# Two transformer blocks in split fp32: the order of the high and low matmuls inside a weight unit

## What is computed

```
def swiglu(h, w_gate, w_up, w_down):
    return (jax.nn.silu(h @ w_gate) * (h @ w_up)) @ w_down
...
proj = h @ w_in
...
return jnp.concatenate([o_attn, o_gla], axis=-1) @ w_out
```

## Time and profile before

| | |
|---|---|
| time, median of 3 runs | 3454.76 us (3454.75 to 3456.53) |
| the profiled execution's own time | 3454.76 us |
| its span, first to last instruction | 3452.9 us |
| TensorE matmul busy | 3390.2 us, 98% of the span |
| TensorE weight load busy | 2946.1 us, 85% |
| VectorE busy | 2366.0 us, 69% |
| ScalarE busy | 1726.5 us, 50% |
| DMA engines, mean busy share | 55% |
| mean granted TensorE clock | 0.994 of full speed |

### The profile page before, as it was taken

One profiled execution on the slowest core, in us unless ns is written; L12 is line 12 of the kernel. 1 busy time (PEld: TensorE's weight loads), 2 busy tenths in 40 slices (PEclk: granted clock), 3 DMA queues, 4 the chain that ended last, 5 costly groups with the idle time before them and its releaser, 6 DMA issues.

```text
span 3452.9 us, 59148 instructions
## 1 busy us (share of the span) xinstructions
PE 3390.2 (98%) x19584; PEld 2946.1 (85%) x19584; DVE 2366.0 (69%) x3637; ACT 1726.5 (50%) x2503; POOL 408.3 (12%) x442
## 2 busy tenths in 40 slices
PE   8999999999999999999999999999999999999999
PEld 7888888887888878888888888888888888888888
DVE  7666666676766856666666677886666668666666
ACT  5444444455444645444444466764444446454454
POOL 1000000011122301000000011210333331101100
PEclk9999999999999999999999999999999999999999
DMA  6665666564554644666566665555554455454545
GB/s 227 187 197 184 192 189 186 177 185 128 152 157 148 194 141 148 193 189 185 186 192 188 187 191 168 187 177 182 152 150 148 146 152 178 152 162 141 162 143 159
DMA packets 167930, 592.48 MB, mean 172 GB/s; under 512 B 18320, under 2 KB 22672, under 8 KB 167712
## 3 DMA queue, kind: packets, MB, share of 16 engines
q1 hardware_dynamic: 166688, 587.11, 55.0%
q10 hardware_dynamic: 1152, 4.19, 0.3%
HBM read 589.14 MB, written 2.10 MB: 171 GB/s over the span
## 4 chain that ended last, share of the span: by engine, by line
PE 50%; issue 11%; DVE 4%; ACT 2%; POOL 1%; DVEq 0%; ACTq 0%; POOLq 0%
PE bank L398 30%; PE bank L397 8%; PE bank L400 7%; PE bank L599 2%; DVE w_low L1218 1%; PE bank L613 1%; POOL rstd L1780 1%; DVE normed L1263 1%; ACT w_high L809 1%; POOL work L1828 1%; DVE residual L1253 0%; DVE increment L1250 0%; PE bank L484 0%; PE bank L491 0%; PE bank L497 0%
## 5 line engine op out<-in xcount | busy, mean ns | idle before, releaser
L398 PE MATMUL bank<-normed,w_high 128*128 128x512 f32 x6208 | 2026.7, 402 | 13.8 <-DVE w_low L1218 10.0
L1218 DVE TENSOR_TENSOR w_low<-w_raw,w_high 128x1024 fp32r<-128x1024 f32 (+1 forms) x1120 | 1372.4, 1234 | 480.6 <-ACT w_high L809 458.3
L809 ACT ACTIVATE w_high<-w_raw 128x1024 fp32r<-128x1024 f32 (+1 forms) x1120 | 1166.1, 1043 | 620.4 <-PE bank L398 601.3
L398 PEld LDWEIGHTS bank<-normed,w_high 128*128 128x128 f32 x6208 | 966.9, 189 | 23.4 <-issue 17.6
L397 PE MATMUL bank<-normed,w_low 128*128 128x256 f32 x3104 | 866.6, 279 | 0.0
L400 PE MATMUL bank<-normed,w_low 128*128 128x256 f32 x3104 | 863.4, 278 | 0.0
L398 PE MATMUL bank<-mixed,w_high 128*128 128x512 f32 x2496 | 796.2, 397 | 6.6 <-DVE increment L1250 6.3
L397 PEld LDWEIGHTS bank<-normed,w_low 128*128 128x128 f32 x3104 | 584.6, 188 | 141.9
L400 PEld LDWEIGHTS bank<-normed,w_low 128*128 128x128 f32 x3104 | 586.5, 189 | 133.9 <-issue 7.7
L826 ACT ACTIVATE parts<-bank 128x256 f32<-128x256 f32 x520 | 198.2, 381 | 822.4 <-PE bank L398 822.3
L1241 DVE TENSOR_TENSOR increment<-bank,parts 128x256 f32<-128x256 f32 x388 | 164.3, 423 | 342.8 <-ACT parts L826 342.5
(11 more groups left out here) (245 smaller groups left out, 2155.1 us busy)
## 6 DMA issues: line engine op xcount, KB each, us to landing
w_raw<-w_hg SPq DMA_DIRECT2D x128, 512.0 KB, 3.5
w_raw<-w_att SPq DMA_DIRECT2D x128, 512.0 KB, 3.6
w_raw<-w_up1a SPq DMA_DIRECT2D x64, 512.0 KB, 4.1
w_raw<-w_up1b SPq DMA_DIRECT2D x64, 512.0 KB, 3.9
w_raw<-w_up2a SPq DMA_DIRECT2D x64, 512.0 KB, 4.1
w_raw<-w_up2b SPq DMA_DIRECT2D x64, 512.0 KB, 4.1
w_raw<-w_rg SPq DMA_DIRECT2D x64, 512.0 KB, 4.3
w_raw<-w_up1c SPq DMA_DIRECT2D x48, 512.0 KB, 4.0
```

The costliest lines, as they stand in the source:

```text
L398: last = nc.tensor.matmul(banks[b][:, :], hi, x, start=starts and k == 0, stop=stop)
L809: A_(wh[slot][:, 0:width], raw[slot][:, 0:width], ACT.Copy).then_inc(wh_done, 1)
L1218: TT(wl[slot][:, 0:width], raw[slot][:, 0:width], wh[slot][:, 0:width].bitcast(F32), ALU.subtract).then_inc(wl_done, 1)
```

## The change

Within a unit every tile now does high, then low, whatever its number. The one exception is the last tile of a unit that closes a group, which does low, then high. The number of matmuls, their operands and their weight loads are the same; only their order inside a unit differs.

```
-                        stop = stops and k == nk - 1
-                        if t % 2:
+                        if stops and k == nk - 1:
                             nc.tensor.matmul(banks[b][:, 0:S], lo, x[:, 0:S], start=False, stop=False)
-                        last = nc.tensor.matmul(banks[b][:, :], hi, x, start=starts and k == 0, stop=stop)
-                        if t % 2 == 0:
+                            last = nc.tensor.matmul(banks[b][:, :], hi, x, start=False, stop=True)
+                        else:
+                            nc.tensor.matmul(banks[b][:, :], hi, x, start=starts and k == 0, stop=False)
                             last = nc.tensor.matmul(banks[b][:, 0:S], lo, x[:, 0:S], start=False, stop=False)
                         t += 1
```

## The result

The changed kernel takes 3481.28 us (median of 4 runs, 3478.25 to 3482.65), the kernel before 3454.76 us in the same comparison (3454.08 to 3456.53). The ratio is 1.0073, 95% interval 1.0061 to 1.0085: 25 us slower (the two medians lie 26.5 us apart, the two profiled executions 24.8). Of 21 executions of the changed kernel on record, one took 5422 us at a mean granted clock of 0.58 and isn't counted. The forecast was 3454.8 us, no change, with a range up to 3478; the result lies 3 us above that range. The profiled execution of the changed kernel took 3479.54 us.

What follows compares the result with a forecast made beforehand. The prediction took TensorE's stream of matmuls to bound the kernel. Reordering was counted as 0: 3454.76 + 0 = 3454.8 us, no change within 0.2% (chance 0.47), range 3438 to 3478 us.

Steps and rivals of the forecast that it cites:

- What bounds the kernel: Whole kernel: as long as TensorE's matmul stream, matmul row busy 3390.2 of 3452.9 us; main-stream tiles 3032 us, 88%.
- The count of turned rounds: Main stream: 3736 of 4352 two-tile rounds turn from L L H H into L H L H.
- the sensitivity: Main stream: 1 ns more a round lengthens the kernel by 3.7 us; 1.85 ns a round is needed to be seen.
- The counts 8088 and 616: Profile sign: lines 397 and 400 trade places; the low matmul behind a high one counts 8088, the other 616.
- The step that failed: Main-stream round: loads covered evenly in either order, so it stays 0.6967 us, a change of 0 us.
- rows 6: Phase with 16-column weights: spacing 0.694 us a round against 0.6967, so loads pace the stream by at most 2.7 ns.
- The bounds from the marks: Main-stream steps between neighbours, H to L 0.231, H to H 0.236 us: from 19 us faster to 20 us slower.
- Rival A: Main stream: two short matmuls in a row hold each other up, so faster: 3445 us, or 3430; chance 0.27.
- Rival B: Main stream: each change of matmul size costs, so 20 us slower, 3475 us, or 37 us, 3492; chance 0.26.
- B's sign in the profile: Main-stream stretch in the profile after: a round of 0.702 us or more.
- The unit's end: 488 units now ending with L: signal within 0.01 us, put at 0, under 2 us; group-closing units end as before.

Runs made afterwards that it cites:

- first stream kernel: TensorE alone, computation left out, 128-tile sections in different orders or operands; H L L H 348.3 ns a tile, H L H L 346.7 or 353.3.
- fifth kernel: Changed kernel without its exception for a group's last tile, so low always last: 3453.04 us against 3455.33 for the kernel before, ratio 1.0011, runs 3447.67 to 3480.62.
- the second: Kernel before with each unit reordered to four high, eight low, four high matmuls: 3463.04 us against 3455.06, ratio 1.0023.
- the kicks: TensorE-only kernel, H L H L sections separated by four same-order matmuls, one L L H H, or eight one-column matmuls: all slow in the first, fast and slow alternating otherwise.
- L681: Section of the second TensorE-only kernel running the changed kernel's group order, with seven L L H H inside: 353.4 ns a tile.

## Why the prediction was wrong

**What bounds the kernel: right.** The time is in the matmul stream, no wait of TensorE moved by more than 1.5 us, and 23.4 of 24.9 us are busy time of the matmul row. The count of turned rounds (3736) and the sensitivity (3.7 us for a nanosecond a round) hold as arithmetic: 25 us are 6.7 ns a round. The counts 8088 and 616 came out too, though the 616 stand on line 396 of the changed kernel, not on 397.

**The step that failed** is this one: "If what a matmul takes depends on itself and on the one load beside it, the round stays 0.6967 us whatever the order: 0 us. I take this value." It does not depend on these alone. The stream H L H L has two steady rates, 346.7 and 353.3 ns a tile, with the same operands, loads and neighbours. So no sum over pairs of neighbours can give its time. The old order showed only one rate, 348.3. In place of the round's 0.6967 us the profiled execution of the changed kernel shows 4.24 / 6 = 0.7067, the slow rhythm.

**The reason given for it** was rows 6: with 16-column loads the spacing is as in the main stream, so the order can give or take little. The premise holds, the conclusion doesn't: with 16-column weights H L H L took 3.3 ns a tile more than H L L H in the first stream kernel (350.0 and 346.7).

**The bounds from the marks** (0.231 and 0.236 us behind an H) I took for rounding, and rightly: by the starts in ns of the trace before, from 100 to 700 us, both steps are 233 ns in the mean, and the two sums over neighbours come to 6 us, one either way. What the means hide is that the old order repeats after eight matmuls: a step from H to L is 230.7 ns in one round and 235.7 in the next, between the same neighbours. That was the sign that a step is no constant of its pair. By chance the upper bound of 20 us, which rests on the marks, is near the 25.

**Rival A** was half right. A fast rhythm below the old rate exists (346.5 ns in the fifth kernel), but not by loads two ahead: in its trace and in the changed kernel's no load starts before the matmul ahead of its own. The Trainium skill's rule of a window from which loads are pulled ahead (TensorE: Matmul & The Clock Gate, section Step-by-step: what each phase is for) is not contradicted, but no run here shows a load more than one matmul ahead.

**Rival B** had the sign and nearly the size, 3475 us against 3481, with a mechanism that fell: changes of kind don't cost as such. The fifth kernel has the most of them and no difference from the kernel before that is clear of noise; the second has two a unit and is slower than it. B's sign in the profile, a round of 0.702 us or more, did come up, so it couldn't tell B from a slow rhythm: luck, not support.

**The unit's end: right.** ScalarE's wait for its slot grew from 601.3 to 611.4 us in a kernel 25 us longer, and TensorE's waits kept their sums within 1.5 us. But the end of the group, where the diff leaves L L H H, was dismissed as the part that "ends as before". It is what breaks the rhythm: without it the same order has a median 28 us lower.

**What stays open.** Why the hardware has two rhythms isn't shown. That L L H H caused the slow rhythm in the profiled execution rests on the fifth kernel, on the kicks and on the count of breaks in its own trace. Other insertions in its place weren't tried, and neither were kicks at the other places of the pattern, apart from those of L681. The fifth kernel's two slowest runs show that the slow rhythm can rule without any L L H H; what picks the rhythm there from run to run stays open.

## What to carry to other kernels

When a kernel is bound by a stream of unequal matmuls, the order of the sizes can matter (0.7% here), and its time can't be summed from the steps of another order: count the matmuls that one long busy window gets through, before and after. A new order whose runs spread more than those of the old one may have two rates; take many runs before believing a gain. An order with one rate (here H L L H) is the safer one. And a break put in always at the same place of a repeating pattern tests that place alone: shift it before calling its effect general.

## What the runs showed of the hardware

With fp32r operands and TensorE alone at work, a 512-column matmul behind another took 226.7 ns and a 256-column one 120.0 with 128-column weights; with 16-column weights it was 231.1 and 113.3, so narrower weights made the long one slower. H L H L ran at 346.7 or at 353.3 ns a tile, and kept the slow rate over 1024 tiles. One L L H H turned it at 12 of 12 places in one stream kernel, where the slow sections all met it at the same place of their pattern; at other places it left the slow rate as it was, seven of seven times in another stream kernel. Eight one-column matmuls turned it 8 of 8 times.
